# A fused two-block network in fp32 on one core: the turning of the attention probabilities, moved from TensorE to VectorE

## The reference, cut to what matters

```python
# layer 0: relative bias, chunks of 64 queries; layer 1: forget gates, blocks of 128 queries
q, k, v, g = h @ w_in                                   # 2048 x 4096 each
for head in range(32):
    sc = q[head] @ k[head].T * 128 ** -0.5 + bias       # or + decay, with the future hidden
    p = softmax(sc, axis=-1)                            # queries x keys
    o[head] = p @ v[head]
x = x + (o * silu(g)) @ w_out
```

## Time and profile before

| | |
|---|---|
| median of 3 runs | 2439.96 us |
| the profiled execution | 2439.27 us, of which the span of its instructions is 2437.5 us |
| granted clock of TensorE | 0.999 of 2.4 GHz |
| PE busy | 2408.9 us (99%) |
| DVE busy | 1759.7 us (72%) |
| ACT busy | 1223.9 us (50%) |
| POOL busy | 307.3 us (13%) |
| DMA | 182 GB/s on the mean |

### The profile page before, as it was taken

One profiled execution on the slowest core, in us unless ns is written; L12 is line 12 of the kernel. 1 busy time (PEld: TensorE's weight loads), 2 busy tenths in 40 slices (PEclk: granted clock), 3 DMA queues, 4 the chain that ended last, 5 costly groups with the idle time before them and its releaser, 6 DMA issues.

```text
span 2437.5 us, 40472 instructions
## 1 busy us (share of the span) xinstructions
PE 2408.9 (99%) x16588; PEld 2151.4 (88%) x16588; DVE 1759.7 (72%) x2629; ACT 1223.9 (50%) x1811; POOL 307.3 (13%) x401
## 2 busy tenths in 40 slices
PE   7999999999999999999999999999999999999998
PEld 7999999888888888888888888888888888888887
DVE  8998797896767676757666669767576757676766
ACT  6555433675544454445444556554454445444545
POOL 1222114432100000000000001200011001000101
PEclk9999999999999999999999999999999999999999
DMA  8666773386666666675766666767676767767764
GB/s 221 176 160 176 199 184 91 104 223 193 189 187 181 193 182 188 189 188 174 188 196 182 193 169 192 195 180 190 195 187 191 185 190 182 195 187 196 186 176 121
DMA packets 758344, 443.31 MB, mean 182 GB/s; under 512 B 28784, under 2 KB 721136, under 8 KB 758160
## 3 DMA queue, kind: packets, MB, share of 16 engines
q1 hardware_dynamic: 752880, 430.16, 63.9%
q0 software_dynamic: 5280, 10.56, 2.9%
HBM read 437.35 MB, written 3.31 MB: 181 GB/s over the span
## 4 chain that ended last, share of the span: by engine, by line
PE 81%; DVE 3%; issue 1%; ACT 0%; DVEq 0%; ACTq 0%
PE bank L295 40%; PE bank L299 20%; PE bank L325 5%; PE bank L326 5%; PE bank L329 5%; PE bank L1886 1%; PE bank L1901 1%; PE bank L1891 1%; PE bank L1885 1%; PE bank L1902 1%; DVE splitb L260 0%; PE bank L275 0%; PE bank L277 0%; PE bank L276 0%; DVE splita L260 0%
## 5 line engine op out<-in xcount | busy, mean ns | idle before, releaser
L295 PE MATMUL bank<-xx,splitb 128*128 128x512 f32 x3328 | 1154.8, 394 | 1.5 <-DVE mix L2183 0.8
L260 DVE TENSOR_TENSOR splitb<-rawb,splitb 128x1024 fp32r<-128x1024 f32 x672 | 837.3, 1255 | 379.4 <-ACT splitb L254 372.0
L254 ACT ACTIVATE splitb<-rawb 128x1024 fp32r<-128x1024 f32 x672 | 702.1, 1055 | 477.9 <-PE bank L299 325.4
L299 PE MATMUL bank<-xx,splitb 128*128 128x256 f32 x3328 | 920.6, 277 | 0.0
L295 PEld LDWEIGHTS bank<-xx,splitb 128*128 128x128 f32 x3328 | 625.0, 188 | 132.5 <-DVE mix L2183 1.1
L299 PEld LDWEIGHTS bank<-xx,splitb 128*128 128x128 f32 x3328 | 625.0, 188 | 2.4
L295 PE MATMUL bank<-oo,splitb 128*128 128x512 f32 x1008 | 343.3, 389 | 0.0
L275 PE MATMUL bank<-xhl,splita 128*128 128x258 f32 (+1 forms) x1040 | 297.7, 286 | 11.8 <-DVE splita L260 10.6
L277 PE MATMUL bank<-xhl,splita 128*128 128x258 f32 (+1 forms) x1040 | 292.9, 282 | 0.0
L276 PE MATMUL bank<-xhl,splita 128*128 128x258 f32 (+1 forms) x1040 | 292.6, 281 | 0.0
L299 PE MATMUL bank<-oo,splitb 128*128 128x256 f32 x1008 | 278.3, 276 | 0.0
(11 more groups left out here) (298 smaller groups left out, 2255.3 us busy)
## 6 DMA issues: line engine op xcount, KB each, us to landing
rawb<-in_a_w_in_dram SPq DMA_DIRECT2D x256, 512.0 KB, 4.8
rawa<-in_w_in_dram SPq DMA_DIRECT2D x130, 512.0 KB, 5.3
rawb<-in_kv_w_dram SPq DMA_DIRECT2D x128, 512.0 KB, 4.8
rawb<-in_b_w_in_dram SPq DMA_DIRECT2D x128, 512.0 KB, 5.4
rawb<-in_a_w_out_dram SPq DMA_DIRECT2D x64, 512.0 KB, 5.2
rawb<-in_b_w_out_dram SPq DMA_DIRECT2D x64, 512.0 KB, 5.2
rawb<-in_w_out_dram SPq DMA_DIRECT2D x32, 512.0 KB, 5.2
table<-in_rel_dram POOLq DMA_DIRECT2D x32, 128.0 KB, 4.8
```

The costliest lines, as they stand in the source:

```text
L254: nc.scalar.activation(self.parts(at, h)[0], self.raw_half(at, h), ACT.Copy).then_inc(hi_ready, 1)
L260: nc.vector.tensor_tensor(lo, self.raw_half(at, h), hi.bitcast(F32), ALU.subtract).then_inc(lo_ready, 1)
L295: nc.tensor.matmul(out, hi[:, w], both(k).rearrange("p a t -> p (a t)"), start=start and k == 0, stop=False)
L299: last = nc.tensor.matmul(out[:, 0:SEQ], lo[:, w], both(k)[:, 0], start=False, stop=stop and k == 7)
```

## The change

The three transposes of a head on TensorE, the PSUM bank that they wrote and ScalarE's copy out of it are gone. In their place VectorE turns the probabilities of a head with 16 instructions. Each takes 32 queries (partitions of `pr`) and 32 keys of each of the 3 blocks of 128 columns, turns the three 32 x 32 blocks, and writes them to the 32 partitions of `pT` that belong to those keys. `pT` has two buffers, by the parity of the head. The inner loop goes over the queries, the outer over the keys, so the input partitions change with every instruction, and the output partitions with every fourth.

```diff
-                    def turn_probs(j):
-                        pe.wait_ge(p_ready, head_no(layer, g, j) * 2 + 2)
-                        for m in range(3):
-                            last = nc.tensor.transpose(PT[:, P * m:P * m + P], pr[:, P * m:P * m + P], ident[:])
-                        last.then_inc(tr_ready, 1)
-
                     def weigh(j):
...
-                        pe.wait_ge(pt_taken, head_no(layer, g, j) + 1)
+                        pe.wait_ge(pt_ready, 2 * head_no(layer, g, j) + 2)
...
                             if j >= 2:
                                 weigh(j - 2)
-                            if 1 <= j <= GH:
-                                turn_probs(j - 1)
                             if j < GH:
                                 scores(j)
...
-                    def take_probs(j):
-                        act.wait_ge(tr_ready, head_no(layer, g, j) + 1)
-                        a(pT[:], PT[:, 0:W3], ACT.Copy).then_inc(pt_taken, 1)
...
+                    def turn_probs(j, h):
+
+                        n = head_no(layer, g, j)
+                        if h == 0:
+                            dve.wait_ge(p_ready, 2 * n + 2)
+                            wait(dve, o_sum, n - 1)
+                        for b in (2 * h, 2 * h + 1):
+                            keys = slice(QB * b, QB * b + QB)
+                            for c in range(NQ):
+                                rows = slice(QB * c, QB * c + QB)
+                                ins = v_.transpose(pT[n % 2][keys].rearrange("k (m q) -> k m q", m=3)[:, :, rows],
+                                                   pr[rows].rearrange("q (m k) -> q m k", m=3)[:, :, keys])
+                        ins.then_inc(pt_ready, 1)
...
                             evacuate("q", j, qT)
+                            if j > LAG:
+                                turn_probs(j - 1, 0)
                             split(place(layer, g, "k", j))
                             evacuate("k", j, kT)
+                            if 1 <= j <= LAG:
+                                turn_probs(j - 1, 0)
+                            if j >= 1:
+                                turn_probs(j - 1, 1)
...
                             gate(j - LAG)
+                            if j == GH - 1:
+                                turn_probs(j, 0)
+                                turn_probs(j, 1)
```

More of the change, by code:

```diff
@@ L1487, in _build @@
         sem("sc_sum"), sem("sc_taken"), sem("max_ready"), sem("exp_ready"), sem("p_ready"))
-    tr_ready, pt_taken, v_taken, o_sum, gate_ready = (
-        sem("tr_ready"), sem("pt_taken"), sem("v_taken"), sem("o_sum"), sem("gate_ready"))
+    pt_ready, v_taken, o_sum, gate_ready = (
+        sem("pt_ready"), sem("v_taken"), sem("o_sum"), sem("gate_ready"))
     inv_col, inv_turned = sem("inv_col"), sem("inv_turned")
@@ L1529, in _build @@
     W3 = 3 * P
-    sc, pr, pT = (sbuf(ph, n, [P, W3]) for n in ("sc", "pr", "pT"))
+    sc, pr = (sbuf(ph, n, [P, W3]) for n in ("sc", "pr"))
     parts = [slice(0, P), slice(P, W3)]
@@ L1541, in _build @@
     f_ones = sbuf(ph, "f_ones", [AH, SEQ])
-    SC, PT, OT, FZ = psum[2:6]
+    SC, _, OT, FZ = psum[2:6]
     OUTS = [OT, FZ]
@@ L1550, in _build @@
     fold_f = sbuf(ph, "fold_f", [P, AH])
+    pT = [sbuf(ph, f"pT{b}", [P, W3]) for b in range(2)]
+    NQ, QB = 4, 32
     f_parts = sc[:, 0:SEQ]
@@ L1900, in weigh @@
                         w = slice(j % VB * P, (j % VB + 1) * P)
-                        nc.tensor.matmul(OUTS[j % 2][:, 0:SEQ], vtm[:, 0, w], pT[:, 0:SEQ], start=True, stop=False)
-                        nc.tensor.matmul(OUTS[j % 2][:, P:SEQ], vtm[:, 1, w], pT[:, SEQ:W3], start=False,
+                        probs = pT[j % 2]
+                        nc.tensor.matmul(OUTS[j % 2][:, 0:SEQ], vtm[:, 0, w], probs[:, 0:SEQ], start=True, stop=False)
+                        nc.tensor.matmul(OUTS[j % 2][:, P:SEQ], vtm[:, 1, w], probs[:, SEQ:W3], start=False,
                                          stop=True).then_inc(o_sum, 1)
@@ L2079, in heads @@
                             split(q)
-                            if j == 2:
-                                take_probs(0)
                             if 1 <= j <= LAG:
@@ L2089, in heads @@
                             ahead(split_hi, at, 0)
-                            if j <= GH:
-                                take_probs(j - 1)
                             ahead(split_hi, at, 1)
```

## The result

| | before | changed kernel |
|---|---|---|
| median | 2440.17 us (5 runs, 2438.97 to 2440.93) | 2543.93 us (5 runs, 2540.04 to 2547.70) |
| profiled execution: span | 2437.5 us | 2546.0 us |

The changed kernel takes 1.0427 times as long, 95% interval 1.0413 to 1.0442. The forecast was 2526; 2544 is 18 us above it and inside the range.

What follows compares the result with a forecast made beforehand. PE, 99% busy, was taken as the bound. Stalls of 98.4 us plus 8.8 for the clock, less 21.1 gained, gave +86.1 on 2439.27: 2525.4, as a median 2526, range 2444 to 2575.

Steps and rivals of the forecast that it cites:

- What leaves: TensorE's three transposes a head, 0.33 us, all on the path: 64 heads gain 21.1 us.
- The price of a turn: One VectorE turn lasts 0.26 us and costs 0.283 start to start, without overlap; bounds 0.17 and 0.36.
- the four copies: VectorE's 32 x 32 copies, each to another 32 partitions: start 0.20 us apart, 0.03 after the one before ends.
- the pair in the same partitions: VectorE instructions touching the same partitions: second starts 0.09 us before the first ends; a turn would cost 0.17.
- The slack: VectorE's four waits in a head in which it is ahead of the others: 3.14 us.
- the round: VectorE's time for a head in mid-group with turns: 18.84 us, against 17.63 for PE without transposes.
- The start: Early heads of a group, 16 turns together behind kT: stalls of 1.11 us at head 2, 3.47 at head 3.
- the prediction's term for the semaphore: PE's scores can start 0.05 us after kT is done.
- The middle: PE waits for kT: heads 4 and 5 stall 1.21 us each, head 7 0.40.
- M: Start of `maxima` counted from the same head's scores matmul; up to 2.06 us no stall, 3.27 after a wait.
- The end: In the first output unit PE waits 4.90 us a group for gT of head 7, done at M + 20.24.
- The clock: Behind idle gaps PE runs at the 1.2 GHz level: 1.1 us for each of 8 gaps, 8.8; bounds 0 and 2.3.

Runs made afterwards that it cites:

- run 1: Changed kernel with all 1024 turns left out (second product reads zeros): 2418.51 us, 0.9911 times before.
- run 3: Changed kernel with all sixteen turns a head reading and writing partitions 0 to 31, output into tiles aside: 2435.10 us, 0.9980 times before.
- run 4: Changed kernel with turns reordered: even heads change the output's quadrant each turn, odd heads both input's and output's: 2543.84 us in one run.
- run 10: Changed kernel with GpSimd's causal mask addition in layer 1 cut to 2 columns in place of 256: 2534.76 us.
- run 2: Changed kernel with eight turns a head in place of sixteen (key blocks 1 and 3 left out): 2431.17 us.
- run 6: Changed kernel with VectorE turning only heads 2, 4 and 5 of each group, TensorE the other five: 2434.02 us, 0.9974 times before.
- run 8: Run 7's split turn for heads 1 to 6 only, TensorE turning 0 and 7, head 1's first moves behind the cross sum copy: 2427.05 us, 0.9942 times before.
- run 7: Changed kernel with one VectorE turn a head inside quadrants, ScalarE moving the sixteen blocks to their quadrants: 2490.56 us, 1.0207 times before.
- run 9: Changed kernel with head 7 of each group turned by TensorE, the other seven by VectorE: 2506.63 us.

## Why the prediction was right, and 18 us short

- **What leaves, 21.1 us:** right. 21.6 by run 1.
- **The price of a turn, 0.283:** right, 0.284, with a duration of 0.27 for 0.26. The choice of the four copies as the nearest rows over the pair in the same partitions decided the forecast. Runs 3 and 4 show its reason: a change of the quadrant on either side holds the next instruction.
- **The slack, 3.14 us, and the round, 18.84:** right in the group that was read and the two behind it (18.84, 18.83). Wrong in layer 1, where rounds reach 19.50 us. The prediction read one group of layer 0 and multiplied by 8. It is wrong in the first group of layer 0 too (19.4 to 20.3). Run 10 puts 9.2 us by the medians, 8.5 by the waits, on one cause in layer 1, GpSimd's addition, which before met VectorE's splits 8 times in 32 and now 18.
- **The start:** against run 1, start to start, head 2 has 0.80 ahead of its unit and 0.65 ahead of its scores, 1.45 for 1.11; head 3 has 0.77 ahead of a split and 2.35 ahead of its scores, 3.12 for 3.47. Together 4.57 for 4.58, which is luck in part: 0.34 too much in one and 0.35 too little in the other. The waits for qT and for the split were not forecast as such; VectorE is late by the same amount wherever PE first asks. From the end of kT's row to L1887 it is 0.15 us (901.47 to 901.62) and not 0.05, the prediction's term for the semaphore.
- **The middle:** 1.21 a head. Where the clock stays up behind head 3 (1144.6), heads 4 and 5 each take 18.83 between scores for 17.65 in run 1, so 1.18. In the group shown head 5 has 939.53 - 921.01 = 18.52, so 0.87, and head 4 hides its stall behind the slow clock. Head 7: 0.40 forecast, PE idle for 0.40, which is 0.57 from start to start, and 1.13 in layer 1. M at head 7: 3.27 forecast, 1000.66 - 997.33 = 3.33.
- **The end, 4.90 in one wait for gT:** the sum was right, the place half right. It came as two waits, 1.89 ahead of the last `weigh` and 2.55 ahead of gT, start to start: 4.44 for 4.90. I had followed gT only and not asked when `pT` of head 7 would be ready, though its sixteen turns were in the same replay. VectorE's queue ended the round as forecast: gT of head 7 was done at M + 19.93, against M + 20.24.
- **The clock, 1.1 us for 8 gaps:** mechanism right, size too small; this is the term that was most off. The clock fell at twelve places, and there the tiles of a unit start 0.64 apart in place of 0.34. By the comparison of starts that is 18.5 us, 1.5 for each place, not 8.8. Splitting the end's wait in two did not save it.
- **Small things, 8.8 us:** not in the prediction. They are spread over the groups, 1 to 2 us in each; what they are I did not isolate.

The pieces: waits 101.9 for 98.4, clock 18.5 for 8.8, the rest 8.8 for 0. That is 22.0 us on the profiled spans; the median of the runs lies 3.8 below the profiled one. That the waits come so near is luck in part: a group was to have 12.3 us of them, the three groups of layer 0 that are like the one read have 10.4 to 11.8, and the other five 12.2 to 15.1.

## What to carry to other kernels

Slack is a property of the queue, not of the busy share: add up the waits in which an engine is truly ahead of the others, over one round, and price new work against that (here 3.14 us, while the page left 28% free). Here work that fitted the slack was all but free in the middle of a pipelined loop (runs 2, 6 and 8) and dear in its last iteration (runs 7 and 9). So in such a loop try to leave the first and the last heads as they were, and check the round of each layer and of its first group. On VectorE keep consecutive small instructions in the same 32 partitions (0.164 against 0.284 us a turn), or turn all quadrants at once and let an engine with free slots do the moves.

## What the runs showed of the hardware that was not expected

- TensorE's clock fell to its lower level behind waits of only 1.9 to 2.7 us, between stretches in which PE was busy, and not behind every such wait (0.51 at 901.6 behind 2.18 us, 1.00 at 1144.6 behind 2.18 and at 1879.6 behind 2.71). A filler of 1.95 us of products that nobody reads kept it up, and made the kernel 9 us faster.
- A turn inside the quadrants over 128 partitions x 384 elements takes 0.57 us, the time of two turns of 32 x 96 that change quadrant, for sixteen times the blocks of one.
- ScalarE's moves of 32 x 96 across quadrants start (1.15 - 0.28) / 3 = 0.29 us apart, no faster than VectorE's turns; they are cheap in run 8 since they lie where ScalarE would have waited (58% busy).
- A turn of the same shape reads 0.23 us long when its neighbours are in its own quadrant and 0.27 when they are not.
